# First attention of a two-block transformer: probabilities scaled before the value products, values as weights, outputs by feature

## The reference, cut to what matters

```python
q = rms_norm(q, g_qn); k = rms_norm(k, g_kn)            # then rope on the last 32 features
logits = jnp.einsum('bqhd,bkhd->bhqk', qi, k) * scale   # causal mask on top
probs = jax.nn.softmax(logits, axis=-1)
o = jnp.einsum('bhqk,bkhd->bqhd', probs, v)
return o.reshape(b, s, MLA_HEADS * MLA_V) @ w_o         # (256 x 1024) @ (1024 x 1024)
```

## Time and profile before

| | us |
|---|---|
| median of 3 runs | 1310.74 (1310.63 to 1311.36) |
| the profiled execution's own time | 1310.61 |
| its span in the profile | 1308.8 |
| PE busy | 1292.2 (99%) |
| DVE busy | 930.3 (71%) |
| ACT busy | 675.9 (52%) |
| first attention with its output product, from the first turn of a head to the next stage | 242.5 to 307.4 |

### The profile page before, as it was taken

The page is one execution under the profiler, slowest core; times in us unless marked ns, Lnnn a source line. Parts: engine busy times, 40 slices in busy tenths (PEclk is TensorE's granted clock), DMA queues, the critical chain, the costliest instruction groups (busy, mean ns, idle before and its releaser), DMA issues.

```text
span 1308.8 us, 16868 instructions
## 1 busy us (share of the span) xinstructions
PE 1292.2 (99%) x6298; PEld 1060.4 (81%) x6298; DVE 930.3 (71%) x1298; ACT 675.9 (52%) x965; POOL 129.6 (10%) x199
## 2 busy tenths in 40 slices
PE   8999999999999999999999999999999999999997
PEld 6888788788888887888888777888888887788886
DVE  6878948886678957577875577567895655655674
ACT  7444527756444536644545566644443735566542
POOL 2000003702000000000001230000000132110000
PEclk9999999999999999999999999999999999999999
DMA  9765545228665554656564643566564496545541
GB/s 304 225 193 192 193 156 174 94 66 252 197 193 199 203 193 161 193 180 199 185 208 145 242 158 111 158 187 193 192 219 144 173 299 211 166 137 177 168 154 33
DMA packets 148785, 236.48 MB, mean 181 GB/s; under 512 B 10087, under 2 KB 103447, under 8 KB 148208
## 3 DMA queue, kind: packets, MB, share of 16 engines
q1 hardware_dynamic: 143600, 222.26, 52.4%
q0 software_dynamic: 4736, 12.96, 3.3%
q10 hardware_dynamic: 384, 0.41, 0.1%
HBM read 233.43 MB, written 4.51 MB: 182 GB/s over the span
## 4 chain that ended last, share of the span: by engine, by line
PE 91%; DVE 3%; ACT 3%; issue 1%; DMA 0%; POOL 0%; SPq 0%; POOLq 0%; ACTq 0%; DVEq 0%
PE acc L626 20%; PE acc L628 20%; PE acc L627 20%; PE acc L659 7%; PE acc L660 7%; PE acc L663 7%; PE misc L702 4%; DVE wl L2042 1%; ACT wh L1512 1%; PE misc L862 1%; PE misc L1321 1%; PE misc L1178 1%; PE acc L843 1%; DMA raw<-in_ffn_w_in_dram 0%; ACT xh L1556 0%
## 5 line engine op out<-in xcount | busy, mean ns | idle before, releaser
L2042 DVE TENSOR_TENSOR wl<-raw,wh 128x2048 fp32r<-128x2048 f32 (+2 forms) x201 | 452.8, 2259 | 172.1 <-ACT wh L1512 171.5
L1512 ACT ACTIVATE wh<-raw 128x2048 fp32r<-128x2048 f32 (+2 forms) x207 | 385.5, 1886 | 122.5 <-PE acc L663 108.2
L626 PE MATMUL acc<-wh,xh 128*128 128x512 f32 (+1 forms) x832 | 324.9, 391 | 2.3 <-DVE xl L2088 1.4
L628 PE MATMUL acc<-wh,xl 128*128 128x512 f32 (+1 forms) x832 | 322.5, 388 | 0.0
L627 PE MATMUL acc<-wl,xh 128*128 128x512 f32 (+1 forms) x832 | 322.2, 387 | 0.0
L626 PEld LDWEIGHTS acc<-wh,xh 128*128 128x128 f32 x832 | 156.2, 188 | 37.2 <-DVE wl L2035 3.5
L628 PEld LDWEIGHTS acc<-wh,xl 128*128 128x128 f32 x832 | 156.2, 188 | 32.2
L627 PEld LDWEIGHTS acc<-wl,xh 128*128 128x128 f32 x832 | 156.3, 188 | 30.9
L1595 ACT ACTIVATE sg<-acc,rstd 128x256 f32<-128x256 f32 x88 | 41.4, 475 | 242.3 <-PE acc L628 242.3
L2218 DVE STREAM_TRANSPOSE aT<-a_n 32x384 f32<-32x384 f32 (+1 forms) x256 | 137.2, 536 | 3.9
L659 PE MATMUL acc<-wh,ah 128*128 128x512 f32 x320 | 125.4, 392 | 0.0
(11 more groups left out here) (378 smaller groups left out, 1624.6 us busy)
## 6 DMA issues: line engine op xcount, KB each, us to landing
raw<-in_ffn_w_in_dram SPq DMA_DIRECT2D x172, 512.0 KB, 4.8
raw<-in_ffn_w_out_dram SPq DMA_DIRECT2D x88, 512.0 KB, 4.2
raw<-in_w_in_dram SPq DMA_DIRECT2D x64, 512.0 KB, 4.7
raw<-in_fox_w_in_dram SPq DMA_DIRECT2D x24, 512.0 KB, 4.5
raw<-in_ple_w_gate_dram SPq DMA_DIRECT2D x16, 512.0 KB, 4.4
raw<-in_mla_w_o_dram SPq DMA_DIRECT2D x8, 512.0 KB, 4.0
raw<-in_fox_w_o_dram SPq DMA_DIRECT2D x8, 512.0 KB, 4.4
raw<-in_w_out_dram SPq DMA_DIRECT2D x8, 512.0 KB, 4.3
```

The source lines that it names most:

```text
L626: pe.matmul(dst, hi, rhs_h, start=first, stop=False)
L628: return pe.matmul(dst, lo, rhs_h, start=False, stop=last)
L1512: act.activation(wh[:, s, 0:n], raw[:, s, 0:n], ACT.Copy).then_inc(hi_done, 1)
L2042: dve.tensor_tensor(wl[:, s, 0:n], raw[:, s, 0:n], wh[:, s, 0:n].bitcast(F32), ALU.subtract)\
```

## The change

In the first attention ACT multiplies the probabilities by their inverse sums, in place, before PE turns them (`scale(j)`, new semaphore `probs_ready`). DVE's `inverse_sums(j)` is a function of its own and stands where ACT needs it; `outputs` is gone. `values(k)` takes two heads: 64 columns of `vn` are the weights, `pT` of both tiles is the moving operand, and the two heads write rows 0 to 63 and 64 to 127 of bank 3, so the result is by feature for both tiles. ACT rounds it (`round_pair`), DVE takes the rest (`rest_pair`), 256 columns per pair, and the output products read them. `turn_first`, `turn_behind`, `round_first`, `rest_first`, `round_behind` and `rest_behind` are gone.

```diff
 PE
                 def probabilities(j):
-                    pe.wait_ge(acc_read[(sq + j) % 2], acc_reads(sq + j))
+                    pe.wait_ge(probs_ready, j + 1)
...
-                def values(j):
-                    pe.wait_ge(m_read[2], base[2] + j + 1)
-                    open_m(3, base[3] + j)
-                    blocks = [[(0, 0)], [(1, 0), (2, 1)]]
...
-                            mm = pe.matmul(M[:, 3, t * HD:(t + 1) * HD], pT[:, j % 2, col * P:(col + 1) * P],
-                                           vn[:, kt, j * HD:(j + 1) * HD],
...
+                def values(k):
+                    pe.wait_ge(m_read[2], base[2] + 2 * k + 2)
+                    open_m(3, base[3] + k)
+                    for lane in range(2):
+                        rows, d = slice(lane * HD, (lane + 1) * HD), (2 * k + lane) * HD
+                        pe.matmul(M[rows, 3, 0:S], vn[:, 0, d:d + HD], pT[:, lane, 0:S], start=True, stop=False)
+                    for lane in range(2):
+                        rows, d = slice(lane * HD, (lane + 1) * HD), (2 * k + lane) * HD
+                        mm = pe.matmul(M[rows, 3, P:S], vn[:, 1, d:d + HD], pT[:, lane, S:3 * P], start=False, stop=True)
+                    mm.then_inc(m_ready[3], 1)
-                def step(i, turn_first, first_products):
+                def step(i):
                     if i < H:
                         turned(i)
...
+                    if i - 1 < H:
+                        scores(i - 1)
+                    if i % 2 == 0:
+                        values(i // 2 - 2)
+                    first_products(i // 2 - 3, i % 2)
+                    probabilities(i - 2)
...
             for i in range(6, H + 2):
-                step(i, turn_first, first_products)
-                if i == H:
-                    turn_behind(0, [(1, 0), (1, 1), (1, 2), (1, 3)])
-            turn_behind(1, [(1, 4), (1, 5), (0, 6), (1, 6)])
...
+                step(i)
+            second_products(0)
+            values(PAIRS - 1)
+            second_products(1)
+            for k in (6, 7):
+                for part in range(2):
+                    first_products(k, part)
+            for k in range(2, DK):
                 if k == 6:
                     turn_h("n2", 2)()
+                second_products(k)
 ACT
+                def scale(j):
+                    act.wait_ge(rin_done, j + 1)
+                    for t, (a, b) in enumerate(((0, P), (P, 3 * P))):
+                        part = probs[:, j % 2, a:b]
+                        e = act.activation(part, part, ACT.Copy, scale=rin[:, t, j:j + 1])
+                    e.then_inc(probs_ready, 1)
+                def round_pair(k):
+                    act.wait_ge(m_ready[3], f[3] + k + 1)
+                    act.activation(xh[:, k, :], M[:, 3, 0:S], ACT.Copy).then_inc(pair_hi, 1)
...
+                    if i - 2 < H:
+                        scale(i - 2)
                     if i < H:
                         copy_queries(i)
+                    if i % 2:
+                        round_pair((i - 5) // 2)
...
                     exponentials(1)
+                    scale(0)
                     copy_queries(4)
                     exponentials(2)
+                    scale(1)
                     square_queries(1, 0)
                     copy_queries(5)
                     exponentials(3)
+                    scale(2)
                     square_queries(1, 1)
+                    scale(3)
+                    round_pair(0)
                     split_half(0)
 DVE
+                def inverse_sums(j):
                     dve.wait_ge(acc_read[(sq + j) % 2], acc_reads(sq + j))
                     dve.reciprocal(rin[:, :, j:j + 1], rs[:, :, j:j + 1]).then_inc(rin_done, 1)
-                def outputs(j):
...
+                def rest_pair(k):
+                    dve.wait_ge(pair_hi, k + 1)
+                    dve.tensor_tensor(xl[:, k, :], M[:, 3, 0:S], xh[:, k, :].bitcast(F32), ALU.subtract)\
                        .then_inc(m_read[3], 1)
```

More of the change, by code:

```diff
@@ L829, in turned, with scores @@
                     mm.then_inc(m_ready[tb], 1)
[L831 removed]
+                def scores(j):
                     tb, tn = j % 2, j // 2
@@ L892, in begin @@
                     probabilities(1)
+                    turned(5)
+                    scores(4)
                     values(0)
-                    turned(5)
                     probabilities(2)
-                    values(1)
-                    scores(4)
                     probabilities(3)
-                    values(2)
-                return begin, step
+                return begin, step, values
             def o_slot(k, n):
@@ L914, in o_weights, with o_high @@
                     pe.wait_ge(quarter_lo, 3 * (k // 2 - 1) + quarter + 1)
[L916 to L931, removed]
+            def o_high(k, t, n):
+                fill = PLAN["mla"][1] + 10 + H + n
+                pe.wait_ge(pair_hi, k + 1)
+                o_weights(k, n)
+                if k == 0 and t == 0:
+                    pe.wait_ge(acc_read[fill % 2], acc_reads(fill - 2 - H))
+                elif k == 0:
+                    open_acc(fill)
+                s, w = o_slot(k, n)
+                x = xh[:, k, t * P:(t + 1) * P]
+                pe.matmul(acc(fill, t), x, wh[:, s, w], start=k == 0, stop=False)
+                pe.matmul(acc(fill, t), x, wl[:, s, w], start=False, stop=False)
@@ L980, in second_low @@
[L980 to L992 removed]
+                    mm = pe.matmul(acc(PLAN["mla"][1] + 10 + H + n, t), xl[:, k, t * P:(t + 1) * P], wh[:, s, w],
+                                   start=False, stop=k == DK - 1)
@@ L994, in _, with first_products, second_products @@
+                    if k == DK - 1 and t == 0:
+                        mm.then_inc(acc_ready, 1)
+                if t and k % 2:
+                    mm.then_inc(w_used, 1)
+            def first_products(k, part):
+                o_high(k, 0, part)
+                if part:
+                    o_low(k, 0)
+            def second_products(k):
+                for n in range(2):
+                    o_high(k, 1, n)
+                o_low(k, 1)
             pe.wait_ge(ident_in, 16)
```

184 lines of the change are left out of this document (33 added, 151 removed).

## The result

The changed kernel takes 1317.37 us (median of 6 runs, 1316.90 to 1318.41), the kernel before 1310.71 (6 runs, 1310.37 to 1311.36): 1.005 times, 95% interval 1.0039 to 1.0061. It is 6.7 us slower; the forecast was 1314.5, with a range of 1311.9 to 1318.5. The profiled execution spans 1315.3 us where before it spanned 1308.8.

A forecast was written before the change was run, and what follows sets the result against it. PE's own work bounds the steady steps before the change. Later starts of +4.7 us by turn 9, less nearly 1 us from removed transposes, gave +3.8 on 1310.6, 1314.4; median 1314.5, range 1311.9 to 1318.5.

The forecast's parts named there:

- rival C: Value products: the two heads don't run beside each other, 3.9 us more in all, 1318.4; chance 0.07.
- rival D: Beginning: PE's clock falls and 6.8 us of work doubles, about half on the chain, +3.4, 1317.9; chance 0.08.
- the scaling: New on ScalarE, two instructions per head: 0.55 us together, with bounds of 0.50 and 0.65.
- the last maxima of the beginning: DVE's maxima of head 4, ahead of the reciprocal of head 3: 0.77 us.
- PE's work: First attention: falls by about 4.5 us, to 5.61 for a steady pair; values of a pair take 0.80.
- The cause: Turning probabilities needed the exponentials alone; now the path is exponentials, reciprocal on DVE, scaling, PE.
- The beginning: Steps 0 to 5, few heads in flight: scores of head 6 +4.1 us; by turn 9, at 269.4, +4.7.
- the first three links: Beginning: probabilities 0 at 249.32, then 3.04 us to probabilities 1 at 252.36, then 3.05 to probabilities 2 at 255.41.
- the fourth: Beginning, from probabilities 2 to 3: 2.68 us through DVE's copy, maxima and reciprocal, to 258.09; before it was 253.68.
- The steady circle: Steady steps: of 0.42 us of saving per pair 0.05 is left; all waits but the bank's are met.
- The bank's circle: Steady steps: a pair's values wait until DVE's rest of the pair before frees their bank; 5.98 us for two heads.
- Behind the heads: After the steps: probabilities 15 wait about 0.7, values of pair 7 about 0.4; next stage at 311.2 against 307.36.

The follow-up runs named there:

- e12: The kernel of e9 with the scaling on ScalarE left out, so outputs stay undivided by the sums; 1307.88 us.
- e1: The changed kernel with the scaling left out, so the result lacks the division by the sums; 1311.89 us.
- e7: The changed kernel with the beginning reordered on PE, ACT and DVE, one more head turned and scored before probabilities 0 and 1; 1313.88 us.
- e11: The changed kernel with an extra copy of the same columns into a spare tile ahead of each scaling, from head 5 on; 1323.48 us.
- e2: The changed kernel with DVE's reciprocal of head 3 moved ahead of the copy of turned probabilities 2 and the maxima of head 4; 1316.27 us.
- e3: The changed kernel with DVE's weight quarter split behind the reciprocal of its step; 1315.81 us.
- e4: The changed kernel with ACT copying the queries of its step before it scales; 1316.82 us.
- e5: The changed kernel with twenty products that nobody reads on PE, in the gap ahead of probabilities 3; 1317.58 us.
- e6: The kernel before with the scaling on ACT added, value products as before, reciprocals at the end of DVE's steps; 1321.71 us.
- e9: The changed kernel with e7's beginning, e3's quarter order, and ScalarE's two half groups of weights moved from the beginning into later steps; 1310.81 us.

## Why the prediction was right in sign and 2.9 us short

**The range: right with luck.** The change was forecast as 3.8 us slower and is 6.7 slower. That is above the forecast's own range, +2.0 to +5.2; the time lies in the stated range only because this took in rivals C (1318.4) and D (1317.9), and neither made the difference: C did not happen, and in the profiled execution, at 1317.04, D cost nothing that could be measured. What came true is the sign, the place and the kind of the loss. Two of its terms were too small, the scaling and the last maxima of the beginning, and one circle of waits was missed.

**PE's work: right.** The value products of a pair go from 269.08 to 269.88, 0.80 as forecast from the earlier trace rows, so the two heads run beside each other and rival C is out. The steady pair's own work of 5.61 is what e12 runs at.

**The cause: right.** The loss is in the wait for the scaled probabilities, most of it in the beginning. Without the scaling (e1) 5.5 of the 6.7 us are gone, and with another order of the beginning and the scaling kept (e7) 3.5.

**The beginning: two terms mis-sized.** I took 0.55 us per head from copies out of PSUM by a constant. The profile shows:

```profile
248.84 0.79 ACT L1686 ACTIVATE probs<-probs,rin 128x128 f32<-128x128 f32 x2
```

0.79, with the next instruction 0.70 behind its start. The upper bound, 0.65, was too low as well. The plain copies of the same columns in e11 take 0.31 and 0.40, the scaled ones 0.39 and 0.49: a scale that is read per partition costs 0.09 more for each instruction, and the copies of the earlier trace rows that I priced it by have none. The Trainium skill, ScalarE: Activation LUTs, What ACT_TABLE_LOAD costs, says that an ACTIVATE with an immediate scale takes 186 ns + 0.833 ns per column, that each pointer operand adds about 93 ns, and that neighbours overlap by about 93. That is 386 + 492 - 93 = 785 ns, an estimate from the page; the trace agrees with 0.79. A row of before had the price too: the query copy of the earlier trace rows, with a scale per partition, takes 0.47 for 256 columns of 96 partitions, where the plain copy of 256 columns in the earlier trace rows takes 0.378 (of 128 partitions).

On the first three links (to probabilities 0, 1 and 2) this made 0.16, 0.17 and 0.17 us, on the fourth 0.43, as there the maxima took 1.02 us until the reciprocal (257.17 to 258.19) and not 0.77. Their last instruction took 0.45 us, where the one of the head before took 0.16; it did so again in e2, e3, e4 and e5, and no run shows why. With 0.2 that the stage began later, probabilities 3 stood at 259.23 against 258.09. Behind it, scores 6 started at 264.65 against 263.15, turn 9 at 270.77 against 269.4. By the steady steps the forecast was 1.3 us short.

**The steady circle: the step that failed.** "The other waits are met: scaled probabilities are ready 0.6 us before PE wants them, keys and queries earlier." The keys are not early. I laid the scaling on ACT's free time and saw that PE would have its result in time, but did not ask what is queued behind it on ACT (the query copy) and who waits for that (DVE's keys, and the reciprocal behind them). The bank's circle that I worked out exists (5.95 in e1 and e4, forecast 5.98), but this one, 6.24, is longer and hides it; e11 lengthened it by one link and e3 and e4 opened it. Four pairs at 0.26 more are 1.0 us. The form of the forecast, a wait of 0.4 ahead of each pair released by DVE's rest, came true to the number without being proof of it: only the distance of the pairs tells the two circles apart.

**Behind the heads: right.** Probabilities 15 wait 0.63 (forecast 0.7), pair 7 waits 0.29 (0.4). The delay then is carried to the end unchanged. 1.3 up to pair 2, 1.0 in the steps and 0.2 between pairs 6 and 7 (5.64 against 5.45) make the next stage 2.56 us later than forecast (313.76 against 311.2); the median run adds 0.3.

**The clock: rival D came and weighed little.** I counted its price from work doubled on the chain, +3.4. In the profiled execution of the changed kernel it lasted 3.3 us, and against e5 it cost nothing that can be measured. In the profiled executions of e3 and e4 it lasted 6 to 7 us, into full work, and took about 1.1; in e6 15 us. The executions of the changed kernel divide with it: those with a mean clock of 0.997 took 1316.9 to 1317.0 us, those with 0.996 took 1317.7 to 1318.4. The Trainium skill, TensorE: Matmul & The Clock Gate, Part 1, has "the default state is throttled, and activity releases the throttle"; the traces agree that a thin stretch is followed by the lower level (0.56 us of work in 3.70, then 0.51), and here the price was what the chain behind it could not hide.

**What stays open.** What of e6's 11 us is the clock, and what the new order alone would give the kernel before. Where e9 needs its 2.9 us for the scaling can be read from the two traces: 1.0 us more than e12 up to pair 2, 1.0 over the four distances from pair 2 to pair 6, and 0.9 from pair 6 to pair 7 (5.68 against 4.79). In the middle part ACT is busy without a gap from 270 to 278.5 us, so there its own row of work, with the halves in it, is the likely bound; no run separates it.

## What to carry to other kernels

When an operation moves to an engine with free time, look not only at who needs its result but at what is queued behind it on that engine, and follow that round until it comes back: a circle through two engines that are each idle for a part of the time (here ACT for 27%, DVE for 19%) can set the pace, and what is added on it counts in full (e11). Price an instruction by a row with the same kinds of operands; a copy with a scale per partition costs more than one by a constant. And a new layout may want a new order: the same arithmetic ran in 1317.4 and in 1310.8 us.

## What the runs showed of the hardware

- ACT, SBUF to SBUF, fp32: a copy of 128 columns 0.31 us and of 256 columns 0.40; with a scale per partition 0.39 and 0.49 (e11).
- PE's clock fell to 0.50 behind thin stretches and stayed there for 3.3 us (after; about as long in e1), 6 to 7 us (e3, e4) or 15 us (e6). The twenty filling products of e5 kept it at 1.00.
- At the lower level 6 us of full PE work held 28 instructions, at 0.91 the next 6 held 45 (e6).
